# A two-block transformer step on one core: second halves of both output products taken block by block with their norms, router per block, first two gathers by the router's own row numbers

## The chip, the cores and the metric

One core of a Trainium2 chip runs the program. The metric is the time of one launch on the device in microseconds, as the median of the runs. TensorE multiplies, VectorE, ScalarE and GpSimd work on rows in SBUF, SyncE issues most of the loads.

## The reference

One sequence of 512 tokens, width 1024, in float32, goes through two different blocks. The first block mixes tokens by a gated linear attention and a state-space scan, multiplies by an output matrix and adds to the residual; then a root-mean-square norm (RMS norm) and a retrieval of single-neuron experts by product keys. The second block mixes by a short convolution and a forgetting attention, multiplies by an output matrix, adds; then a norm and a mixture of 32 experts with a router.

```python
h = h + mixed @ w_out                          # first output product
n2 = rmsnorm(h, norm_ffn_w)
h = h + peer_ffn(n2, ...)                      # starts with n2 @ w_query, 16 tiles of 128 features
...
x = x + token_mixer(rmsnorm_2(x, g_mix), ...)  # ends with m @ w_out_2, second output product
hf = rmsnorm_2(x, g_ffn)
pg = softmax(hf @ w_router_group); le = hf @ w_router_expert
x = x + hier_moe(hf, ...)                      # top 1 of 4 groups, top 2 of its 8 experts
```

## The kernel before, in words

The program is one instruction stream for each engine, written out by hand and held together by semaphores: the order on each engine is the order of its code, and an instruction whose semaphore is late holds up all behind it on the same engine.

**Numbers as pairs.** Float32 operands are split into a bf16 high half (ScalarE, a copy) and a bf16 low half (VectorE, operand minus high half). A product is three bf16 matmuls, high-high, high-low and low-high (`mm3`, L684 to L687).

**Weights.** All weights come as chunks of 1 MB (128 x 2048 float32), loaded by SyncE in the order of use into a ring of four slots `w_st`; ScalarE writes `w_hi` (L1176), VectorE `w_lo` (L1586), each up to three chunks ahead (`ahead(n)`), as the slot's last users allow (`used(n)`). In the expert stage the ring has twelve slots, some of them in buffers of earlier stages (`a_hi`, `a_lo`, `xn`), and the splits stand at L1505 and L2134. The loads into `a_hi` and `a_lo` wait for the router's last matmul, those into `xn` wait until GpSimd has read `xn` and both first gathers have landed.

**Tokens.** The 512 tokens are four blocks of 128. A token-major product (`token_tiles`, L701) covers 512 output columns for all four blocks with two chunks: for chunk 0 all four blocks, then for chunk 1 all four blocks, 12 matmuls of 512 columns each time. Each output product is two such halves. VectorE adds the result to the residual (L1759, L2108), and behind the second half each block is normalised: ScalarE square (L1186) and root (L1188), VectorE reciprocal (L1596) and scaling (L1600) into `xn`.

**Turning.** What follows wants features on the partitions. `transpose_rows` (L720, its matmul L730) turns a block with eight 128x128 transposes in two groups of four, each group in one of two PSUM banks; ScalarE writes the group's high half into `a_hi` (L1195), VectorE its low half into `a_lo` (L1610). A group waits until the bank's group before it is split (`tp_lo`). Before the change all four blocks are turned behind the whole product (uses 2 and 5), and the next product waits for all of them:

```python
token_tiles(C_WOUT + 2, 0, a_hi, a_lo)
transpose_rows(2)
pe.wait_ge(tp_lo, 3 * KT)
...
token_tiles(C_WO2 + 2, 4, m_split[:, :, 0, :], m_split[:, :, 1, :])
pe.drain().then_inc(moe_mm, RING)
transpose_rows(5)
pe.wait_ge(tp_lo, 6 * KT)
```

**Query stage.** Behind the first product come 16 query tiles (`feature_tile`, L689): each 24 matmuls over all 512 tokens, two tiles to a weight chunk, in banks 4 to 7 in turn. VectorE's low half is at L1824, ScalarE's high half at L1307.

**Router and gathers.** Behind the second product the router takes 24 matmuls of 36 columns for each block. GpSimd meanwhile stores each normalised block as a bf16 pair in DRAM (L618, L620, L622). VectorE picks experts, ranks the tokens and writes the row numbers of every expert, `row_i` (L2231). GpSimd waits for them, copies two columns to `idx` (L646), drains, and gathers 64 rows each for the first two experts (L626); TensorE turns the gathered rows (L1091) and starts on expert 0. Later gathers are issued one expert ahead, by `idx` (copies at L630).

Of the kernel before, what the change touches and what calls it, by code (L numbers as in the profile page):

```python
# [15 lines left out]
P = 128  # L16
# [110 lines left out]
def build_program(nc, w_all, x_in, cols_in, small_in, rows_in, out):  # L127
    ctx = ExitStack()
    with ctx:  # L129
# [340 lines left out]

        block = ctx.enter_context(nc.Block())
# [48 lines left out]
        def _(pool):  # L520
# [104 lines left out]
            def gather(p):  # L625
                pool.indirect_dma_start(x_g[0:CAP, p, :, :].rearrange("p a d -> p (a d)"), None, x_dram,  # L626
                                        bass.IndirectOffsetOnAxis(ap=idx[0:CAP, p:p + 1], axis=0)).then_inc(xe_ld[p], 16)
# [52 lines left out]
        def _(pe):  # L680
# [8 lines left out]
            def feature_tile(f, n, half, r_hi, r_lo, bank=None):  # L689
# [30 lines left out]
            def transpose_rows(use, by_block=True):  # L720

                for n in range(KT):
# [3 lines left out]
                    for m in range(4):  # L726
# [3 lines left out]
                        last = pe.transpose(ps[:, g % 2, m * P:(m + 1) * P], xn[:, tb, kt * P:(kt + 1) * P], ident[:, :])  # L730
# [148 lines left out]
            for m in range(2 * N_QUERY):  # L879
                feature_tile(F_QUERY + m, C_QUERY + m // 2, m % 2, a_hi, a_lo)  # L880
# [190 lines left out]
            last.then_inc(rt_mm, 1)  # L1071
# [95 lines left out]
        def _(act):  # L1167
# [22 lines left out]
            def transposed(use, weight=None, dst=a_hi, blocks=range(TB)):  # L1190

                for n in range(2 * blocks[0], 2 * blocks[-1] + 2):
                    act.wait_ge(tp_done, KT * use + n + 1)
                    if weight is None:
                        act.activation(dst[:, (n % 2) * 4:(n % 2) * 4 + 4, (n // 2) * P:(n // 2 + 1) * P],  # L1195
                                       ps[:, n % 2, :].rearrange("p (k t) -> p k t", k=4), ACT.Copy).then_inc(tp_hi, 1)
# [1176 lines left out]
```

## Time and profile before

| | us |
|---|---|
| median of the runs (2842.1 to 2848.28) | 2842.36 |
| the profiled execution | 2843.14 |
| its span, first to last instruction | 2841.5 |
| TensorE busy | 2652.2 (93%) |
| VectorE busy | 2021.4 (71%) |
| ScalarE busy | 1294.2 (46%) |
| GpSimd busy | 654.1 (23%) |

The profile is of one execution. Times are counted from the span's start; PE is TensorE's matmuls, PEld its weight loads, DVE VectorE, ACT ScalarE, POOL GpSimd, SP SyncE. Matmuls are pipelined: one that is shown with 0.38 us starts a good 0.2 us behind the one before, so their cost is the distance of their starts. In brackets stands how long the engine was idle before a row, and what ended that; "issue" is idle time for which the profile shows no wait.

### The profile page before, as it was taken

Reading aid. Unit: us, or ns where it says so; the run is one execution under the profiler, and the core shown is the slowest. Engines: PE = TensorE matmul, PEld = TensorE weight load, DVE = VectorE, ACT = ScalarE, POOL = GpSimd, SP = SyncE. Lnnn points to the kernel's source line nnn. Section 1 sums busy time; section 2 is a strip of 40 time slices with the busy share of each in tenths; the row PEclk is TensorE's granted clock in tenths of the full one; section 3 lists DMA queues with packets and bytes.
Section 4 is the critical chain, followed back from the end, with each engine's and each line's share of the span. In section 5 each row is a group of like instructions: output and inputs, shape, how many; then the busy total and the mean of one; then the engine's idle time right before and its main releaser. Section 6 shows DMA issues by size and latency. Waiting matters only on the chain. (4 is left out here: it accounts for less than half of the span.)

```text
span 2841.5 us, 39775 instructions
## 1 busy us (share of the span) xinstructions
PE 2652.2 (93%) x14118; PEld 1344.3 (47%) x14323; DVE 2021.4 (71%) x3310; ACT 1294.2 (46%) x1379; POOL 654.1 (23%) x480
## 2 busy tenths in 40 slices
PE   6988999999999999999999699999999599999994
PEld 3464444444455554444444344455554355555552
DVE  4544688886788885888888754366643588888885
ACT  5432323323444444333333333344431478888884
POOL 0000000000001013888888400000000332223221
PEclk9988999999999999999999899999999799999997
DMA  5201234443375658999999522212113399999994
GB/s 193 104 30 60 97 112 156 148 147 149 139 225 180 226 178 283 347 366 362 365 369 362 218 89 104 89 60 75 68 53 147 145 394 390 397 398 399 394 397 158
DMA packets 129053, 609.05 MB, mean 214 GB/s; under 512 B 17328, under 2 KB 33712, under 8 KB 79296
## 3 DMA queue, kind: packets, MB, share of 16 engines
q1 hardware_dynamic: 57312, 411.62, 38.3%
q0 software_dynamic: 45024, 149.00, 15.0%
q10 hardware_dynamic: 26624, 47.19, 4.9%
q8 instruction: 58, 0.95, 0.1%
q14 instruction: 35, 0.29, 0.0%
HBM read 539.59 MB, written 68.16 MB: 214 GB/s over the span
## 5 line engine op out<-in xcount | busy, mean ns | idle before, releaser
L686 PE MATMUL ps<-a_lo,w_hi 128*128 128x512 bf16 x1654 | 628.5, 380 | 6.3 <-DVE a_lo L1610 1.8
L687 PE MATMUL ps<-a_hi,w_lo 128*128 128x512 bf16 x1653 | 627.9, 380 | 1.4
L685 PE MATMUL ps<-w_hi,arena 128*128 128x512 bf16 (+1 forms) x1583 | 602.2, 380 | 16.3 <-ACT arena L1522 14.6
L685 PE MATMUL ps<-a_hi,w_hi 128*128 128x512 bf16 x1604 | 609.5, 380 | 2.4 <-ACT arena L1419 0.7
L686 PE MATMUL ps<-w_lo,arena 128*128 128x512 bf16 (+1 forms) x1582 | 601.4, 380 | 3.0 <-DVE arena L1945 2.2
L687 PE MATMUL ps<-w_hi,arena 128*128 128x512 bf16 (+1 forms) x1583 | 601.5, 380 | 0.9
L1834 DVE TENSOR_TENSOR w_lo<-w_st,w_hi 128x2048 bf16<-128x2048 f32 x128 | 293.2, 2290 | 184.0 <-ACT w_hi L1316 151.7
L1316 ACT ACTIVATE w_hi<-w_st 128x2048 bf16<-128x2048 f32 x128 | 244.4, 1909 | 321.8 <-PE ps L687 315.1
L590 POOL DMA_INDIRECT arena<-act_dram,h_idx x128 | 270.6, 2114 | 39.9 <-issue 39.9
L1322 ACT ACTIVATE xn<-ps 128x512 f32<-128x512 f32 x128 | 76.4, 597 | 426.8 <-PE ps L687 426.8
L1586 DVE TENSOR_TENSOR w_lo<-w_st,w_hi 128x2048 bf16<-128x2048 f32 x67 | 153.1, 2288 | 153.2 <-ACT w_hi L1176 152.9
L685 PEld LDWEIGHTS ps<-w_hi,arena 128*128 128x128 bf16 (+1 forms) x1600 | 166.2, 104 | 198.8 <-issue 17.7
L687 PEld LDWEIGHTS ps<-a_hi,w_lo 128*128 128x128 bf16 x1680 | 164.8, 98 | 199.3 <-issue 1.9
L685 PEld LDWEIGHTS ps<-a_hi,w_hi 128*128 128x128 bf16 x1680 | 164.9, 98 | 190.2 <-issue 4.1
L687 PEld LDWEIGHTS ps<-w_hi,arena 128*128 128x128 bf16 (+1 forms) x1600 | 166.4, 104 | 180.5 <-issue 1.7
L686 PEld LDWEIGHTS ps<-a_lo,w_hi 128*128 128x128 bf16 x1680 | 164.8, 98 | 182.9 <-issue 1.3
L686 PEld LDWEIGHTS ps<-w_lo,arena 128*128 128x128 bf16 (+1 forms) x1600 | 166.2, 104 | 176.6 <-issue 1.6
L566 POOL DMA_DIRECT2D act_dram<-xn x64 | 34.1, 533 | 752.3 <-ACT xn L1322 741.8
L1920 DVE TENSOR_SCALAR xn<-iota_b,arena 128x128 bf16<-128x128 bf16 x768 | 175.6, 312 | 0.0
L1176 ACT ACTIVATE w_hi<-w_st 128x2048 bf16<-128x2048 f32 x67 | 127.2, 1903 | 106.0 <-PE ps L687 106.0
L2134 DVE TENSOR_TENSOR w_lo<-w_st,w_hi 128x2048 bf16<-128x2048 f32 x64 | 145.9, 2282 | 28.0 <-ACT w_hi L1505 28.0
L2134 DVE TENSOR_TENSOR w_lo<-arena,w_hi 128x2048 bf16<-128x2048 f32 x64 | 144.7, 2281 | 4.2 <-ACT w_hi L1505 4.2
(392 smaller groups left out, 3749.8 us busy)
## 6 DMA issues: line engine op xcount, KB each, us to landing
w_st<-in_w_all SPq DMA_DIRECT2D x260, 1024.0 KB
arena<-in_w_all SPq DMA_DIRECT2D x64, 1024.0 KB
act_dram<-xn POOLq DMA_DIRECT2D x64, 512.0 KB, 2.9
xn<-in_w_all SPq DMA_DIRECT2D x32, 1024.0 KB, 9.1
arena<-act_dram ACTq DMA_DIRECT2D x64, 384.0 KB
gate_dram<-arena POOLq DMA_DIRECT2D x7, 3072.0 KB, 19.3
arena<-gate_dram ACTq DMA_DIRECT2D x64, 336.0 KB
a_hi<-in_w_all SPq DMA_DIRECT2D x16, 1024.0 KB, 9.1
```

The costliest lines, as they stand in the source:

```text
L566: pool.dma_start(act_dram[i * 8 + c], u_st[:, c % 2, :, :].rearrange("p j t -> p (j t)")).then_inc(u_stored[c % 2], 16)
L590: pool.indirect_dma_start(act_0[:, k:k + 1], None, acts, bass.IndirectOffsetOnAxis(ap=h_idx[:, k:k + 1], axis=0)).then_inc(act_ld[k // ROW ...
L685: pe.matmul(dst, l_hi, r_hi, start=start, stop=False)
L686: pe.matmul(dst, l_hi, r_lo, start=False, stop=False)
L687: return pe.matmul(dst, l_lo, r_hi, start=False, stop=stop)
L1176: act.activation(dst, w_st[:, n % RING, :], ACT.Copy).then_inc(w_hi_done, 1)
L1316: act.activation(w_hi[:, s, :], w_st[:, s, :], ACT.Copy).then_inc(w_hi_done, 1)
L1322: act.activation(u_st[:, c % 2, t, :], ps[:, t, :], ACT.Gelu).then_inc(u_out, 1)
L1586: dve.tensor_tensor(lo_n, w_st[:, n % RING, :], hi_n, ALU.subtract).then_inc(w_lo_done, 1)
L1834: dve.tensor_tensor(w_lo[:, s, :], w_st[:, s, :], w_hi[:, s, :], ALU.subtract).then_inc(w_lo_done, 1)
L1920: last = dve.tensor_scalar(oh_a[:, at % 2, r, part, :], iota_b[:, :], c_slot[:, 0, k:k + 1], c_slot[:, 2 + part, k:k + 1], ALU.is_equal, A ...
L2134: dve.tensor_tensor(w_lo[:, s, :], moe_st[k % MOE_RING], w_hi[:, s, :], ALU.subtract).then_inc(w_lo_done, 1)
```

## The change

The second half of each output product goes block by block (`block_tiles`): both chunks for block 0, then both for block 1, and so on, so both chunks are wanted from the start. The turns of finished blocks (`turn`) stand among them on TensorE. In the first product block 0 is turned behind block 2 and block 1 behind block 3, in banks 6 and 7 (`TURN_2`), and query tiles 0 and 1 are computed in parts: blocks 0 and 1 (256 columns), block 2, block 3, each when its block is split, with turn 3 in between. In the second product block 0 is turned behind block 1 and so on, and the router takes blocks 0 to 2 ahead of the turn of block 3. ScalarE and VectorE normalise each block before they split the turn of the block before it. Chunk C_WOUT + 6 = C_QUERY + 1 (query tiles 2 and 3) is no longer split ahead of the norms but behind the last turn. The bank of a query tile is 4 + m % 4 on ScalarE and VectorE too; `transposed` gets the argument `bank`. GpSimd's first pass gathers by `row_i` itself, without copy and drains, and drains once before the third gather's row numbers are used.

```diff
--- before
+++ after
@@ -643,11 +645,15 @@
 
             def first(r):
                 pool.wait_ge(rt_row, r + 1)
-                pool.tensor_tensor(idx[0:CAP, 0:2], row_i[0:CAP, 0:2], zero_i[0:CAP, :], ALU.add)
-                pool.drain()
-                gather(0)
-                gather(1)
-                pool.drain()
+                if isinstance(r, int):
+                    gather(0, row_i)
+                    gather(1, row_i)
+                else:
+                    pool.tensor_tensor(idx[0:CAP, 0:2], row_i[0:CAP, 0:2], zero_i[0:CAP, :], ALU.add)
+                    pool.drain()
+                    gather(0)
+                    gather(1)
+                    pool.drain()
                 next_rows(0, 2)
                 pool.drain()
...
@@ -686,17 +692,35 @@
                 pe.matmul(dst, l_hi, r_lo, start=False, stop=False)
                 return pe.matmul(dst, l_lo, r_hi, start=False, stop=stop)
 
-            def feature_tile(f, n, half, r_hi, r_lo, bank=None):
+            def feature_tile(f, n, half, r_hi, r_lo, bank=None, cols=slice(0, T), done=True):
 
                 chunk(n)
                 if bank is None and f >= 4:
                     pe.wait_ge(ft_out, f - 3)
-                dst = ps[:, 4 + f % 4 if bank is None else bank, :]
+                dst = ps[:, 4 + f % 4 if bank is None else bank, cols]
                 for kt in range(KT):
                     w = slice(half * D + kt * P, half * D + (kt + 1) * P)
-                    last = mm3(dst, w_hi[:, n % RING, w], w_lo[:, n % RING, w], r_hi[:, kt, :], r_lo[:, kt, :],
+                    last = mm3(dst, w_hi[:, n % RING, w], w_lo[:, n % RING, w], r_hi[:, kt, cols], r_lo[:, kt, cols],
                                kt == 0, kt == KT - 1)
-                last.then_inc(ft_done, 1)
+                if done:
+                    last.then_inc(ft_done, 1)
+
+            def block_tiles(n, bank, l_hi, l_lo, tb):
+
+                rows = slice(tb * P, (tb + 1) * P)
+                for part in range(2):
+                    if tb == 0:
+                        chunk(n + part)
+                    for k in range(4):
+                        kt = part * 4 + k
+                        w = slice(k * 512, (k + 1) * 512)
+                        last = mm3(ps[:, bank + tb, :], l_hi[:, kt, rows], l_lo[:, kt, rows],
+                                   w_hi[:, (n + part) % RING, w], w_lo[:, (n + part) % RING, w],
+                                   kt == 0, kt == KT - 1)
+                    if part == 1:
+                        last.then_inc(tok_done, 1)
+                    elif tb == TB - 1:
+                        last.then_inc(tok_half, 1)
 
             def token_tiles(n, bank, l_hi, l_lo, split=None, before=0):
...
@@ -861,11 +885,30 @@
             pe.wait_ge(ssd_yd, TB)
             transpose_rows(1, by_block=False)
             token_tiles(C_WOUT, 4, a_hi, a_lo, tp_lo, KT)
-            token_tiles(C_WOUT + 2, 0, a_hi, a_lo)
-
-
-            transpose_rows(2)
+
+            def turn(use, tb, bank=0):
+                transpose_rows(use, groups=range(2 * tb, 2 * tb + 2), bank=bank)
+
+            for tb in range(TB):
+                block_tiles(C_WOUT + 2, 0, a_hi, a_lo, tb)
+                if tb >= 2:
+                    turn(2, tb - 2, TURN_2)
+
+            def query_part(m, blocks):
+                first, end = blocks
+                feature_tile(F_QUERY + m, C_QUERY + m // 2, m % 2, a_hi, a_lo, 4 + m % 4, slice(first * P, end * P), end == TB)
+
+            turn(2, 2, TURN_2)
+            pe.wait_ge(tp_lo, 2 * KT + 4)
+            query_part(0, (0, 2))
+            query_part(1, (0, 2))
+            turn(2, 3, TURN_2)
+            pe.wait_ge(tp_lo, 2 * KT + 6)
+            query_part(0, (2, 3))
+            query_part(1, (2, 3))
             pe.wait_ge(tp_lo, 3 * KT)
+            query_part(0, (3, 4))
+            query_part(1, (3, 4))
 
             def scores(unit, h, rows):
 
@@ -876,8 +919,10 @@
                                keys_hi[:, q, :], keys_lo[:, q, :], True, True)
                 last.then_inc(s_done, 1)
 
-            for m in range(2 * N_QUERY):
-                feature_tile(F_QUERY + m, C_QUERY + m // 2, m % 2, a_hi, a_lo)
+            for m in range(2, 2 * N_QUERY):
+                if m >= 4:
+                    pe.wait_ge(ft_out, F_QUERY + m - 3)
+                query_part(m, (0, 4))
                 if m % 2 and 3 <= m < 3 + 2 * EARLY:
                     pe.wait_ge(ft_out, F_QUERY + m - 1)
...
@@ -1057,18 +1102,25 @@
                     pe.wait_ge(mix_done, j - 1)
                 feature_tile(ao_out(j) - 1, C_AO + j, 1, c_hi, c_lo, bank=7 - 2 * (j % 2))
             token_tiles(C_WO2, 0, m_split[:, :, 0, :], m_split[:, :, 1, :], mix_lo)
-            token_tiles(C_WO2 + 2, 4, m_split[:, :, 0, :], m_split[:, :, 1, :])
-
-            pe.drain().then_inc(moe_mm, RING)
-
-            transpose_rows(5)
-            pe.wait_ge(tp_lo, 6 * KT)
             for tb in range(TB):
+                block_tiles(C_WO2 + 2, 4, m_split[:, :, 0, :], m_split[:, :, 1, :], tb)
+                if tb == TB - 1:
+                    pe.drain().then_inc(moe_mm, RING)
+                if tb:
+                    turn(5, tb - 1)
+
+            def router(tb):
+                pe.wait_ge(tp_lo, 5 * KT + 2 * tb + 2)
                 for kt in range(KT):
                     rows, w = slice(tb * P, (tb + 1) * P), slice(O_R + kt * SM_R, O_R + (kt + 1) * SM_R)
                     last = mm3(ps[:, 2, tb * SM_R:(tb + 1) * SM_R], a_hi[:, kt, rows], a_lo[:, kt, rows], small_hi[:, w], small_lo[:, w],
                                kt == 0, kt == KT - 1)
-            last.then_inc(rt_mm, 1)
+                return last
+
+            for tb in range(TB - 1):
+                router(tb)
+            turn(5, TB - 1)
+            router(TB - 1).then_inc(rt_mm, 1)
 
             pe.wait_ge(rt_pick, 1)
             pe.matmul(ps[:, 3, 0:TB * NE].rearrange("p (t e) -> p t e", e=NE), tri_le[:, :], e_any, start=True, stop=False)
...
@@ -1290,21 +1342,20 @@
                 act.drain()
             act.activation(sd[:, 0:TB * SG], ss[:, 0:TB * SG], ACT.Sqrt, scale=1.0 / (SJ * SP_), bias=eps[:, :]).then_inc(ssd_sd, 1)
             transposed(1, lambda kt: col("gla_norm") if kt < 4 else col("ssd_norm", kt - 4))
-            for g in range(2):
-                ahead(C_WOUT + 2 * g)
-                act.wait_ge(tok_half, G_WOUT + g + 1)
-                ahead(C_WOUT + 2 * g + 1)
+            ahead(C_WOUT)
+            act.wait_ge(tok_half, G_WOUT + 1)
+            ahead(C_WOUT + 2)
 
 
             for tb in range(TB):
-                if tb == TB - 1:
-                    transposed(2, blocks=[0])
                 norm(1, tb, res_done, tb + 1)
-            transposed(2, blocks=range(1, TB))
+                if tb:
+                    transposed(2, blocks=[tb - 1], bank=TURN_2)
+            transposed(2, blocks=[TB - 1], bank=TURN_2)
             for m in range(2 * N_QUERY):
...
@@ -1752,20 +1802,16 @@
 
             for g in range(2):
                 ahead(C_WOUT + 2 * g)
-                ahead(C_WOUT + 2 * g + 1)
                 for tb in range(TB):
                     dve.wait_ge(tok_done, TB * (G_WOUT + g) + tb + 1)
                     s = slice(g * 512, (g + 1) * 512)
                     last = dve.tensor_tensor(res[:, tb, s], res[:, tb, s], ps[:, 4 - 4 * g + tb, :], ALU.add)
                     if g == 1:
                         last.then_inc(res_done, 1)
+                        normalise(1, tb)
                         if tb:
-                            normalise(1, tb - 1)
-            transposed(2, blocks=[0])
-            normalise(1, TB - 1)
-
-
-            transposed(2, blocks=range(1, TB))
+                            transposed(2, blocks=[tb - 1], bank=TURN_2)
+            transposed(2, blocks=[TB - 1], bank=TURN_2)
             def best_keys(h):
 
```

ScalarE's and VectorE's parts for the second product are changed in the same way as those shown for the first.

## Rows read from the trace of the kernel before

**Rows 1.** Waits of TensorE, 2190 to 2257 us: us in total, times, longest
```profile
PE ps L1091 <- DMA arena<-x_dram,arena: 12.5, 1, 12.5
```

**Rows 2.** Windows: busy us of PE, PEld, DVE, ACT, POOL; granted clock; DMA share; GB/s
```profile
284.90:308.50 23.60, 17.68 (x80) 9.74 (x80) 13.84 (x16) 10.21 (x15) 3.76 (x7) 0.78 0.30 112
...
2243.30:2257.40 14.10, 1.03 (x16) 0.87 (x16) 2.98 (x4) 1.19 (x2) 4.15 (x4) 0.50 0.12 37
2300.00:2400.00 100.00, 97.39 (x570) 50.62 (x569) 88.79 (x53) 81.56 (x66) 29.74 (x18) 1.00 1.01 392
2700.00:2800.00 100.00, 93.80 (x538) 48.43 (x536) 87.03 (x52) 79.35 (x63) 16.57 (x12) 1.00 0.83 326
```

**Rows 3.** Timeline of TensorE behind the first output product: start, us, line, operation
```profile
284.93 1.04 PE L730 MATMUL ps<-ident,xn 128*128 128x128 f32 x8
...
290.77 1.97 PE L730 MATMUL ps<-ident,xn 128*128 128x128 f32 x8 [1.60 <-DVE a_lo L1610]
...
297.08 0.63 PE L686 MATMUL ps<-a_lo,w_hi 128*128 128x512 bf16 x1 [1.82 <-DVE a_lo L1610]
297.50 0.63 PE L687 MATMUL ps<-a_hi,w_lo 128*128 128x512 bf16 x1
...
308.34 0.38 PE L687 MATMUL ps<-a_hi,w_lo 128*128 128x512 bf16 x1
308.56 0.38 PE L685 MATMUL ps<-a_hi,w_hi 128*128 128x512 bf16 x1
```

**Rows 4.** Timeline of VectorE in the same stretch
```profile
276.79 2.29 DVE L1586 TENSOR_TENSOR w_lo<-w_st,w_hi 128x2048 bf16<-128x2048 f32 x1 [8.09 <-ACT w_hi L1176]
...
285.13 0.69 DVE L1759 TENSOR_TENSOR res<-res,ps 128x512 f32<-128x512 f32 x1 [0.31 <-PE ps L687]
285.74 0.16 DVE L1596 RECIPROCAL rstd<-sd 128x1 f32<-128x1 f32 x1
285.97 1.28 DVE L1600 SCALAR_TENSOR_TENSOR xn<-res,rstd,row 128x1024 f32<-128x1024 f32 x1
...
295.93 0.69 DVE L1610 TENSOR_TENSOR a_lo<-ps,a_hi 128x512 bf16<-128x512 f32 x1 [0.16 <-ACT a_hi L1195]
```

**Rows 5.** Timeline of ScalarE in the same stretch
```profile
286.54 1.06 ACT L1186 ACTIVATE xn<-res 128x1024 f32<-128x1024 f32 x1
...
287.75 0.29 ACT L1188 ACTIVATE sd<-ss,eps 128x1 f32<-128x1 f32 x1
...
294.44 0.60 ACT L1195 ACTIVATE a_hi<-ps 128x512 bf16<-128x512 f32 x1 [1.08 <-PE ps L730]
...
295.79 3.70 ACT L1176 ACTIVATE w_hi<-w_st 128x2048 bf16<-128x2048 f32 x2
```

**Rows 6.** Timeline of TensorE: router's first and last matmul, the first expert's rows
```profile
2226.69 0.19 PE L685 MATMUL ps<-small_hi,a_hi 128*128 128x36 bf16 x1 [1.42 <-DVE a_lo L1610]
...
2229.24 0.20 PE L687 MATMUL ps<-small_hi,a_lo 128*128 128x36 bf16 x1
...
2255.57 1.03 PE L1091 MATMUL ps<-ident_b,arena 64*128 64x64 bf16 x16 [12.47 <-DMA arena<-x_dram,arena]
```

**Rows 7.** Timeline of VectorE: block 3's rows, the row numbers, the next chunk's low half
```profile
2217.29 2.84 DVE L1600 SCALAR_TENSOR_TENSOR xn<-res,rstd,row 128x1024 f32<-128x1024 f32 x1
...
2243.14 0.18 DVE L2231 CAST arena<-ps 64x32 int32<-64x32 f32 x1 [0.55 <-PE ps L1141]
2243.25 2.27 DVE L2134 TENSOR_TENSOR w_lo<-w_st,w_hi 128x2048 bf16<-128x2048 f32 x1
```

**Rows 8.** Timeline of GpSimd: the program's first gather, then the expert stage
```profile
1103.85 1.04 POOL L594 DMA_INDIRECT arena<-in_w_all,v_idx  x1 [0.31 <-issue]
...
2243.41 2.16 POOL L646 TENSOR_TENSOR arena<-arena,zero_i 64x2 int32<-64x2 int32 x1 [11.86 <-DVE arena L2231]
2251.69 0.95 POOL L626 DMA_INDIRECT arena<-x_dram,arena  x1 [6.12 <-issue]
...
2287.21 2.80 POOL L626 DMA_INDIRECT arena<-x_dram,arena  x1 [0.16 <-issue]
```

More of the change, by code:

```diff
@@ L623, in _, with gather @@
             pool.wait_ge(x_st, 16 * TB)
-            def gather(p):
+            def gather(p, rows=idx):
                 pool.indirect_dma_start(x_g[0:CAP, p, :, :].rearrange("p a d -> p (a d)"), None, x_dram,
-                                        bass.IndirectOffsetOnAxis(ap=idx[0:CAP, p:p + 1], axis=0)).then_inc(xe_ld[p], 16)
+                                        bass.IndirectOffsetOnAxis(ap=rows[0:CAP, p:p + 1], axis=0)).then_inc(xe_ld[p], 16)
             def next_rows(i, c):
@@ L718, in token_tiles, with transpose_rows @@
                             last.then_inc(tok_half, 1)
-            def transpose_rows(use, by_block=True):
-                for n in range(KT):
+            def transpose_rows(use, by_block=True, groups=range(KT), bank=0):
+                for n in groups:
                     g = KT * use + n
@@ L729, in transpose_rows @@
                             pe.wait_ge(xn_done, TB * use + tb + 1)
-                        last = pe.transpose(ps[:, g % 2, m * P:(m + 1) * P], xn[:, tb, kt * P:(kt + 1) * P], ident[:, :])
+                        last = pe.transpose(ps[:, bank + g % 2, m * P:(m + 1) * P], xn[:, tb, kt * P:(kt + 1) * P], ident[:, :])
                     last.then_inc(tp_done, 1)
@@ L1188, in norm, with transposed @@
                 act.activation(sd[:, tb:tb + 1], ss[:, tb:tb + 1], ACT.Sqrt, scale=1.0 / D, bias=eps[:, :]).then_inc(sd_done, 1)
-            def transposed(use, weight=None, dst=a_hi, blocks=range(TB)):
+            def transposed(use, weight=None, dst=a_hi, blocks=range(TB), bank=0):
                 for n in range(2 * blocks[0], 2 * blocks[-1] + 2):
@@ L1486, in _ @@
             mix_high(KT - 1)
-            for g in range(2):
-                ahead(C_WO2 + 2 * g)
-                act.wait_ge(tok_half, G_WO2 + g + 1)
-                ahead(C_WO2 + 2 * g + 1)
+            ahead(C_WO2)
+            act.wait_ge(tok_half, G_WO2 + 1)
+            ahead(C_WO2 + 2)
             for tb in range(TB):
-                if tb == TB - 1:
-                    transposed(5, blocks=[0])
                 norm(4, tb, res_done, TB + tb + 1)
-            transposed(5, blocks=range(1, TB))
+                if tb:
+                    transposed(5, blocks=[tb - 1])
+            transposed(5, blocks=[TB - 1])
             def hi_of(r, i, k):
@@ L1602, in normalise, with transposed @@
                     dve.drain().then_inc(row_used, 1)
-            def transposed(use, weight=None, dst_hi=a_hi, dst_lo=a_lo, blocks=range(TB)):
+            def transposed(use, weight=None, dst_hi=a_hi, dst_lo=a_lo, blocks=range(TB), bank=0):
                 for n in range(2 * blocks[0], 2 * blocks[-1] + 2):
@@ L1609, in transposed @@
                         part = (slice(None), slice((n % 2) * 4, (n % 2) * 4 + 4), slice((n // 2) * P, (n // 2 + 1) * P))
-                        dve.tensor_tensor(dst_lo[part], ps[:, n % 2, :].rearrange("p (k t) -> p k t", k=4), dst_hi[part], ALU.subtract).then_inc(tp_lo, 1)
+                        dve.tensor_tensor(dst_lo[part], ps[:, bank + n % 2, :].rearrange("p (k t) -> p k t", k=4), dst_hi[part], ALU.subtract).then_inc(tp_lo, 1)
                     else:
@@ L2103, in _ @@
                 ahead(C_WO2 + 2 * g)
-                ahead(C_WO2 + 2 * g + 1)
                 for tb in range(TB):
@@ L2110, in _ @@
                         last.then_inc(res_done, 1)
+                        normalise(4, tb)
                         if tb:
-                            normalise(4, tb - 1)
-            transposed(5, blocks=[0])
-            normalise(4, TB - 1)
-            transposed(5, blocks=range(1, TB))
+                            transposed(5, blocks=[tb - 1])
+            transposed(5, blocks=[TB - 1])
             def rows_of_pass(r):
```

7 lines of the change are left out of this document (4 added, 3 removed).

## The prediction

> **What bounds the kernel now.** TensorE is busy for 93% of the span (table above), so I began with who waited for whom on it, in the two stretches that change. The longest wait there is 12.5 us, for the rows of the first gather [rows 1]; the others are of a few us each, for the low halves of transposed rows. Next I took the windows [rows 2]. From the end of the first output product to query tile 2 TensorE is busy 17.7 of 23.6 us at a mean granted clock of 0.78; between the router's row numbers and the first expert TensorE is busy 1.03 of 14.1 us, and the DMA share is 0.12: nothing else runs there either. Between 2300 and 2400 TensorE is 97% busy and the DMA engines are full too, but between 2700 and 2800 the DMA share is already 0.83 with TensorE still busy, so the weight stream is done ahead of TensorE and the expert stage goes by TensorE. All stages hang on the one before by semaphores only. What is saved in either place is therefore saved at the end, if the next wait doesn't take it.
>
> **First place: the first output product.** A turn is the eight transposes of one block of 128 tokens. Durations: a 512-column matmul at the high level (2.4 GHz, granted clock 1.00) starts every 0.216 us; at the low level (1.2 GHz, 0.50) every 0.427 us; eight transposes take 1.04 us, 1.97 at the low level [rows 3]. One block of the second half is 24 matmuls, 5.18 us; the four blocks cost 20.7 us in either order. VectorE: residual add 0.69 (the next starts after 0.61), reciprocal and its drain 0.23, normalise 1.28, low half of a transposed group 0.69, low half of a weight chunk 2.29 [rows 4]. ScalarE: from the square to the end of the root 1.50, high half of a group 0.60, two chunks' high halves 3.70, so 1.9 each [rows 5].
> Before: the transposes start at 284.93, directly behind the product, query tile 0 at 296.65 (one matmul ahead of the 297.08 in the row), and tile 2 at 308.56 [rows 3]. The gap is 11.7 us, two of the four turns at the low level; and tiles 0 and 1 take 11.9 us where 48 matmuls at 0.216 are 10.4, so 1.5 us more went to the low level.
> After, from the start of the second half at 264.4: blocks 0 to 2 end at 279.9, turn 0 at 281.0, block 3 at 286.2, turn 1 at 287.2. VectorE is the queue to follow: it takes the residual add of block 2 only after turn 0 has been split (282.4), and that of block 3 only after turn 1 has (288.7). Turn 2 waits for turn 1's buffers: 288.1 to 289.2. The residual of block 3 is ready at 289.3, its root at 290.95, its rows at 292.5, turn 2's low half at 293.7. Meanwhile TensorE does the 256-column parts of query tiles 0 and 1: 2 x 2.6 us, 289.2 to 294.4. Turn 3: 294.4 to 295.5. The third blocks' parts (2 x 1.3): to 298.1; turn 3 is split at 296.9, so the last parts follow without a wait to 300.8. Narrow matmuls cost by their columns: 96 matmuls of 36 columns, each with a new stationary tile, take 2.55 us [rows 6], so setting one costs no more than 0.027 us and hides under 128 columns.
> The weight chunk of tiles 2 and 3 was split under the product before (276.79 in [rows 4]); now it is split after turn 3: high half 296.1 to 298.0, low half to 300.4. That is 0.4 us ahead of need: I cost it at nothing, and its cover is thin. The two chunks behind it come under tiles 2 and 3; SyncE's load of the chunk five later goes out some 21 us later than before, and is needed only at tile 10. Gain: 308.56 - 300.8 = **7.8 us**. Bounds: no more than 8.7 (TensorE without any wait: 20.7 + 4.2 + 10.6 us); no less than 3 (the four last short parts at the low level, 2 us each later or so, and the chunk late).
>
> **Second place: the second output product and the router.** The second half starts at 2192.5. Before, its 20.7 us end at 2213.3 and the router's 96 matmuls run from 2226.69 to 2229.44 [rows 6]; their result is read right behind. VectorE normalised block 3 at 2217.29 for 2.84 instead of 1.28 us [rows 7], beside a GpSimd subtraction.
> After: turns 0 and 1 stand among the blocks, +2.1 us, block 3 ends at 2215.5. Its residual 2216.1, root 2217.9, rows at 2219.5 (GpSimd is in the store of block 2 by then, so 1.28 and not 2.84), turn 2's low half 2220.75. TensorE has turned block 2 and done the router of blocks 0 and 1 by 2218.1 and waits; router 2 ends at 2221.5, turn 3 at 2222.5 to 2223.4 by the clock, its low half 1.4 us later, the last router block takes 0.65 to 0.8. The result is whole at 2225.0 (2224.6 to 2225.8). Gain: **4.4 us**, bounds 2.5 (block 3's rows slow again, and the low level) and 5.5. GpSimd's four stores start earlier and are out by 2226; the row numbers come some 13 us later, so that wait stays hidden. The 14 us of routing arithmetic are untouched.
>
> **Third place: the gathers.** Before, the row numbers are written at 2243.32 (2243.14 + 0.18), GpSimd copies them (2.16 us), its drain and what follows leave it idle for 6.12 us, and the first gather is issued at 2251.69 for 0.95 us; TensorE starts on the gathered rows at 2255.57, that is 2.93 us after the first issue ended [rows 6 to 8]. Now the gathers read the row numbers themselves. Ahead of gathers elsewhere the idle time is 0.31 us after a wait [rows 8]. But VectorE starts a chunk's low half at 2243.25 for 2.27 us [rows 7], and a gather in the expert loop, issued beside such subtractions, takes 2.80 us instead of 0.95 [rows 8]. So: issue ends 2.3 + 0.9 = 3.2 us after the row numbers, not 9.3. Gain **6.1 us**; bounds 8.0 (no such lengthening) and 0 (the idle time just moves ahead of the gather, and the lengthening comes on top). The copy for the third gather comes after both, and that gather isn't needed for two experts. SyncE's loads into xn wait for both gathers; the second then lands some 6 us earlier as well, so the stream shifts with TensorE. Its lead at the end [rows 2] covers the rest.
> The trace's 6.12 us has a rule that speaks against this part. The Trainium skill, "GPSIMD Engine Reference", section Instruction dispatch, says that the first call to a freshly loaded GpSimd kernel additionally pays a load of about 6 us with no visible instruction; by it the idle time would belong to the gather and stay. The trace doesn't decide: at 1103.85 the first of all gathers waited only 0.31 us, but it followed other DMA work and not arithmetic [rows 8].
>
> **Sum.** 7.8 + 4.4 + 6.1 = 18.3 us. The profiled execution took 2843.14 us, 0.8 above the median: 2843.1 - 18.3 = 2824.8 against it, and 2824.0 against the median. What a measurement of this kernel can tell from no change is about 0.3%, 8.5 us.
>
> **Rivals.**
> (a) The 6 us ahead of the first gather stay. GpSimd would wait 2.16 us less (the copy), VectorE's subtraction would be over, so only about 2.2 us are gained there: 7.8 + 4.4 + 2.2 = 14.4, 2828. For it: nothing that the profile names fills the 6.12 us. Against: the gather at 1103.85, and the later gathers behind a copy wait only 0.16 us [rows 8]. By the skill's rule just named it would go so. 20%.
> (b) The deferred chunk split isn't covered: ScalarE takes it behind turn 3 and TensorE waits some 4 us before tile 2. 14 us in all, 2828. For it: a margin of 0.4 us. Against: every duration in that chain is measured, and one would have to be off by several us. 10%.
> (c) Only the last block counts. Its own chain (residual, norm, turn, split, router) stays as long as it was, and the two turns among the blocks come on top, in both places (2 x 2.1 us): 6.1 - 4.2, no more than 2 us gained, 2840.5, no change. For it: the end of both products is set by block 3 alone. Against: that chain was 16 us long while its own links, summed from [rows 4 to 6], are about 8; the rest was other blocks' work queued in front on ScalarE and VectorE. 6%.
> (d) Slower: the short parts with waits between them leave TensorE at the low level, and it stays there in the query stage. Each 512-column matmul then costs 0.211 us more; from 87 of them (under four tiles) the whole gain is gone, from 127 the kernel is measurably slower; over all 16 query tiles it is 384 x 0.211 = 81 us, less the 18: 2905. For it: turn 2 went at the low level 6 us after turn 0 had gone at the high one [rows 3]. Against: tiles 0 and 1 lost only 1.5 us to it before it was back [rows 3], and after the change there is less idle time, not more. 4%.
>
> **Numbers.** Forecast as summed 60%, (a) 20%, (b) 10%, (c) 6%, (d) 4%. Faster by over 0.3%: 0.90; within 0.3%: 0.06; slower by over 0.3%: 0.04. Range: the bounds of the three terms taken one at a time reach from 2822 to 2830, all three at their best give 2820; (a) and (b) lie inside, and both at once give 2832. So 2820 to 2832.
>
> **What would show it.** Right: one 8-transpose group between blocks 2 and 3 near 280 at 1.04 us; query tile 2 starts near 300.8, directly behind tile 1's last part, at 0.216 us spacing throughout; the router's last matmul near 2217.2 (2225.0 less the 7.8 gained before); the first gather starts under 0.5 us after the row numbers are written and takes near 2.8 us; the expert stage keeps its length. Wrong: a GpSimd idle time of about 6 us ahead of the first gather (a); TensorE idle before tile 2 until w_lo (b); TensorE idle for over 8 us between block 3's end and the last router block (c); a granted clock of 0.50 after 302 (d); or, if expert waits now name w_lo or a weight load, the stream was the bound.

## The result, and the profile after

| | before | after |
|---|---|---|
| median of the runs, us | 2842.62 (2842.1 to 2848.28) | 2827.72 (2825.69 to 2829.11) |
| ratio | | 0.9944 [0.993, 0.9957] |
| the profiled execution, us | 2843.14 | 2825.69 |
| its span, us | 2841.5 | 2823.9 |

The median before includes the runs made beside the changed kernel. The 27 runs of the kernel before beside the first experiments lie in two groups, near 2842.5 and near 2847.6 us, so a difference of two medians is good to a few us only, and the terms are better read from traces. The change gains 14.9 us by the medians and 17.45 us between the two profiled executions; the one profiled after is the fastest of its four. The forecast was 2824.0, in a range of 2820 to 2832.

The page's busy times, after:

```profile
span 2823.9 us, 39964 instructions
...
PE 2648.8 (94%) x14215; PEld 1348.0 (48%) x14419; DVE 2019.6 (72%) x3310; ACT 1293.6 (46%) x1379; POOL 651.2 (23%) x479
```

TensorE does nearly the same work (2648.8 against 2652.2 us busy). So the time is idle time that went, and it has to be found by place.

**Where the 17.6 us of the span went.** I took the same events in both traces and subtracted. Each figure is how much earlier the event comes after the change:

| event | before | after | earlier by |
|---|---|---|---|
| last residual add of the first product's first half | 264.41 | 263.85 | 0.56 |
| high half of query tile 2 copied | 313.94 | 305.20 | 8.74 |
| first tile of the retrieval loop | 387.46 | 378.72 | 8.74 |
| last tile of the retrieval loop | 1102.12 | 1095.07 | 7.05 |
| last residual add of the second product's first half | 2192.59 | 2185.16 | 7.43 |
| router's result read | 2229.47 | 2218.06 | 11.41 |
| row numbers written | 2243.32 | 2231.92 | 11.40 |
| TensorE starts on the gathered rows | 2255.57 | 2237.88 | 17.69 |
| end | 2841.50 | 2823.95 | 17.55 |

The first place gives 8.74 - 0.56 = 8.2 us, the second 11.41 - 7.43 = 4.0, the third 17.69 - 11.40 = 6.3, in all 18.5. The 0.56 is no part of the three: the four other kernels with the first product as it was show the same add at 263.1 to 265.9 us. Between the first and the last tile of the retrieval loop, in code that the change doesn't touch, 1.7 us are lost.

**First place.** TensorE from block 2's end to query tile 2, the timeline that answers to [rows 3]:

```profile
279.19 1.04 PE L754 MATMUL ps<-ident,xn 128*128 128x128 f32 x8
...
285.24 1.04 PE L754 MATMUL ps<-ident,xn 128*128 128x128 f32 x8
...
287.26 1.25 PE L754 MATMUL ps<-ident,xn 128*128 128x128 f32 x8 [0.98 <-DVE a_lo L1660]
288.35 0.27 PE L691 MATMUL ps<-a_hi,w_hi 128*128 128x256 bf16 x1
...
293.59 1.04 PE L754 MATMUL ps<-ident,xn 128*128 128x128 f32 x8
...
299.76 0.22 PE L693 MATMUL ps<-a_hi,w_lo 128*128 128x128 bf16 x1
300.04 0.38 PE L692 MATMUL ps<-a_lo,w_hi 128*128 128x512 bf16 x1
```

The first two rows are turns 0 and 1 among the blocks, 1.04 us each. Turn 2 waits 0.98 us for its banks, the 256-column parts run from 288.35, turn 3 goes at the high level, and query tile 2 starts at 299.8 (one matmul ahead of the row at 300.04), without an idle time between. VectorE in the same stretch, answering to [rows 4]:

```profile
286.51 1.29 DVE L1660 TENSOR_TENSOR a_lo<-ps,a_hi 128x512 bf16<-128x512 f32 x2 [1.07 <-ACT a_hi L1247]
287.71 0.68 DVE L1808 TENSOR_TENSOR res<-res,ps 128x512 f32<-128x512 f32 x1
...
290.21 1.28 DVE L1650 SCALAR_TENSOR_TENSOR xn<-res,rstd,row 128x1024 f32<-128x1024 f32 x1
...
297.14 6.70 DVE L1636 TENSOR_TENSOR w_lo<-w_st,w_hi 128x2048 bf16<-128x2048 f32 x3 [1.00 <-ACT w_hi L1228]
```

Turn 1 is split and only then comes block 3's residual add (287.71). The row at 297.14 is three weight chunks' low halves one behind the other: the first, which tile 2 needs and whose split was put off, ends a third of the way in, at 299.4. The windows, in the columns of [rows 2], first the turning, then the stretch between the row numbers and the first expert, then the two stretches of the expert stage:

```profile
264.00:299.60 35.60, 34.52 (x267) 22.54 (x267) 20.92 (x25) 16.12 (x24) 3.77 (x7) 1.00 0.22 75
...
2232.00:2239.60 7.60, 1.03 (x16) 0.88 (x16) 2.77 (x3) 1.07 (x2) 3.88 (x3) 0.50 0.25 69
2300.00:2400.00 100.00, 97.39 (x569) 50.66 (x568) 88.79 (x54) 81.58 (x66) 29.84 (x18) 1.00 1.01 396
```

TensorE is busy for 34.5 of 35.6 us at a granted clock of 1.00; before, the turning alone went at 0.78 [rows 2]. The expert stage is as it was.

**Second place.** TensorE in the second product, answering to the first rows of [rows 6]:

```profile
2208.18 1.07 PE L754 MATMUL ps<-ident,xn 128*128 128x128 f32 x8 [0.26 <-issue]
2209.09 0.18 PE L691 MATMUL ps<-small_hi,a_hi 128*128 128x36 bf16 x1
...
2213.24 0.19 PE L691 MATMUL ps<-small_hi,a_hi 128*128 128x36 bf16 x1 [2.79 <-DVE a_lo L1660]
2213.86 1.85 PE L754 MATMUL ps<-ident,xn 128*128 128x128 f32 x8
...
2217.12 0.21 PE L691 MATMUL ps<-small_hi,a_hi 128*128 128x36 bf16 x1 [1.42 <-DVE a_lo L1660]
...
2217.83 0.20 PE L693 MATMUL ps<-small_hi,a_lo 128*128 128x36 bf16 x1
```

TensorE waits 2.79 us for block 2's low half, and turn 3 then takes 1.85 us instead of 1.04: most of it went at the low level.

**Third place.** GpSimd and, below it, TensorE, answering to [rows 8] and [rows 6]:

```profile
2232.19 2.75 POOL L628 DMA_INDIRECT arena<-x_dram,arena  x1 [13.77 <-DVE arena L2273]
2235.25 0.93 POOL L628 DMA_INDIRECT arena<-x_dram,arena  x1 [0.30 <-issue]
```

```profile
2237.88 1.03 PE L1143 MATMUL ps<-ident_b,arena 64*128 64x64 bf16 x16 [6.18 <-DMA arena<-x_dram,arena]
```

The first gather starts 0.27 us after the row numbers are written; the 6.12 us of [rows 8] have not moved ahead of it. It takes 2.75 us, beside this row of VectorE:

```profile
2231.85 2.27 DVE L2176 TENSOR_TENSOR w_lo<-w_st,w_hi 128x2048 bf16<-128x2048 f32 x1
```

TensorE's wait for the rows is 6.2 us instead of 12.5 [rows 1].

**Where the 1.7 us went.** The stretch of 4 us at the entry to the retrieval loop, before the change and after it, columns as above:

```profile
384.00:388.00 4.00, 2.59 (x16) 1.45 (x18) 1.13 (x2) 3.73 (x3) 0.00 (x0) 1.00 0.52 219
```

```profile
377.00:381.00 4.00, 3.77 (x11) 1.52 (x12) 2.26 (x2) 2.99 (x2) 0.00 (x0) 0.58 0.13 53
```

The granted clock falls to 0.58 on average, and about eight matmuls start 0.427 us apart instead of 0.216: 8 x 0.211 = 1.7 us. The idle time ahead of it, a wait of 1.93 us before the change and 1.94 after it, is in both traces.

### The profile page after: what moved, and what is told of

Same layout as the page of the kernel before. It is cut to its first block and busy times, and to the rows that moved or that the text cites. A ratio compares the mean times of both kernels' runs of the same rounds, so it can differ in the third digit from the quotient of the medians.

```text
span 2823.9 us, 39964 instructions
## 1 busy us (share of the span) xinstructions
PE 2648.8 (94%) x14215; PEld 1348.0 (48%) x14419; DVE 2019.6 (72%) x3310; ACT 1293.6 (46%) x1379; POOL 651.2 (23%) x479
## 5 line engine op out<-in xcount | busy, mean ns | idle before, releaser
L692 PE MATMUL ps<-a_lo,w_hi 128*128 128x512 bf16 (+2 forms) x1686 | 632.2, 376 | 4.5 <-issue 0.7
L693 PE MATMUL ps<-a_hi,w_lo 128*128 128x512 bf16 (+2 forms) x1686 | 632.0, 376 | 1.4
L691 PE MATMUL ps<-a_hi,w_hi 128*128 128x512 bf16 (+2 forms) x1636 | 613.4, 376 | 2.4 <-ACT arena L1470 0.7
```

What stands on the lines that cost most here:

```text
L691: pe.matmul(dst, l_hi, r_hi, start=start, stop=False)
L692: pe.matmul(dst, l_hi, r_lo, start=False, stop=False)
L693: return pe.matmul(dst, l_lo, r_hi, start=False, stop=stop)
```

## The experiments

Three things were to be settled: whether the three terms are those of the three parts and add up; what the 6.12 us ahead of the first gather are; and whether the query parts or the turns among the blocks carry the first term.

**The change again**, five rounds, with no edit, to see what repeats.

> The changed kernel once more, with five rounds. By its one trace the three places gain 8.2, 4.0 and 6.3 us, 18.5 together, and 1.7 us are lost where TensorE enters the expert-retrieval loop at the lower clock for some 3.5 us, which the kernel before did not show. Theory: that loss is a matter of the single execution, so the trace of this run may show it or not, the three gains repeat within 0.3 us, and the median of more runs lies 15 to 18 us below the kernel before. Rival: the loss comes with the change every time; then this trace shows the clock at 0.5 near 378 us again and the median stays near 15 us below.

Measured: 2826.21 us (2825.51 to 2830.8, five runs); ratio 0.9942 [0.9929, 0.9956]. The trace repeats each term: 8.2, 4.0 and 6.3, and the 1.7 us lost at the loop's entry:

```profile
377.30:381.30 4.00, 3.84 (x10) 1.45 (x12) 2.38 (x2) 2.87 (x2) 0.00 (x0) 0.57 0.05 20
```

The expectation isn't settled by it: the loss was there again, as its rival says, and the median is 17.1 us below that of the kernel before (2843.35 beside these runs), as its theory says.

**The first product's part alone.** The kernel before with only these edits (and those of ScalarE and VectorE that belong to use 2):

```diff
-            token_tiles(C_WOUT + 2, 0, a_hi, a_lo)
-            transpose_rows(2)
+            for tb in range(TB):
+                block_tiles(C_WOUT + 2, 0, a_hi, a_lo, tb)
+                if tb >= 2:
+                    turn(2, tb - 2, TURN_2)
...
+            query_part(0, (0, 2))
+            query_part(1, (0, 2))
+            turn(2, 3, TURN_2)
...
```

> Only the first output product with its norms, turns and split query tiles is changed. Theory (the places add up): query tile 2 starts 8.2 us earlier, the second product's router and the gathers keep their length, 2834 to 2836 us in all. Rival (a stall moves: later stages are held by something else): tile 2 starts earlier but the time is within 3 us of the kernel before.

Measured: 2836.32 us (2835.68 to 2841.54, ten runs), ratio 0.9977 [0.9968, 0.9986]. In the trace query tile 2 comes 8.98 us earlier, of which 0.80 stand upstream: 8.2. The router and the gathers keep their length. The 1.7 us at the loop's entry are lost here too, and the median lies 0.3 us above the range that was expected.

**The second product's part alone.**

```diff
-            token_tiles(C_WO2 + 2, 4, m_split[:, :, 0, :], m_split[:, :, 1, :])
-            pe.drain().then_inc(moe_mm, RING)
-            transpose_rows(5)
...
+                block_tiles(C_WO2 + 2, 4, m_split[:, :, 0, :], m_split[:, :, 1, :], tb)
+                if tb == TB - 1:
+                    pe.drain().then_inc(moe_mm, RING)
+                if tb:
+                    turn(5, tb - 1)
...
+            for tb in range(TB - 1):
+                router(tb)
+            turn(5, TB - 1)
+            router(TB - 1).then_inc(rt_mm, 1)
```

> Only the second output product and the router are changed. Theory: the router's result is read 4.0 us earlier, the row numbers and gathers follow unchanged, 2838 to 2839 us. Rival (only the last block's chain counts, and two turns stand in front of it): no gain or 2 us slower, 2842 to 2845 us.

Measured: 2838.85 us (2837.98 to 2844.91, ten runs), ratio 0.9984 [0.9975, 0.9994]. In the trace the router's result comes 5.19 us earlier, 1.14 of them upstream: 4.05. The loop's entry goes at a clock of 1.00, as before the change:

```profile
384.00:388.00 4.00, 3.61 (x20) 1.90 (x22) 1.55 (x1) 3.69 (x3) 0.00 (x0) 1.00 0.30 123
```

**The gathers' part alone.**

```diff
-                pool.tensor_tensor(idx[0:CAP, 0:2], row_i[0:CAP, 0:2], zero_i[0:CAP, :], ALU.add)
-                pool.drain()
-                gather(0)
-                gather(1)
-                pool.drain()
+                if isinstance(r, int):
+                    gather(0, row_i)
+                    gather(1, row_i)
...
```

> Only the first two gathers take the router's row numbers directly; all else as before. Theory: the first gather starts 0.3 us after the row numbers instead of 8.4, takes 2.75 us instead of 0.95 beside VectorE's subtraction, and TensorE starts on its rows 6.3 us earlier: 2836 us. Rival (the idle time belongs to the gather's first call and was gone in the changed kernel for another reason, the earlier stores): 6 us of idle time ahead of the first gather, 2840 us.

Measured: 2838.72 us (2834.92 to 2841.41, ten runs), ratio 0.9975 [0.9966, 0.9985]. The profiled execution reaches the row numbers 4.2 us late, in code that the edit doesn't touch, and TensorE starts on the rows 2.06 us early, so the part gives 6.24 us:

```profile
2247.78 2.75 POOL L626 DMA_INDIRECT arena<-x_dram,arena  x1 [11.78 <-DVE arena L2235]
```

The 4.2 us can be placed: 1.45 are lost up to the first product's first half, 1.3 more up to query tile 2, where the low level lasts longer than in [rows 2] (0.71 over the same 23.6 us, instead of 0.78), and 1.7 at the loop's entry; 0.3 come back behind it.

```profile
286.35:309.95 23.60, 17.88 (x74) 9.48 (x74) 13.84 (x16) 10.22 (x15) 3.76 (x7) 0.71 0.30 112
```

The three parts alone give 8.2 + 4.05 + 6.24 = 18.5 us, what the whole change shows in the same places. They neither help nor hinder one another. By the medians, against 2843.35 us, they gain 7.0, 4.5 and 4.6 us, 16.1 together, and the whole change 17.1. The 1.7 us are lost here as well, and this kernel has the first product as it was: the loss can come without the first part.

**What are the 6.12 us?** Three theories were held against one another: C, the copy as GpSimd's first arithmetic of its kind; G, the first gather itself; D, the drain between them, which has to wait for something that the transfers issued before have left. The first test adds a copy of the same kind to the kernel before, into a tile of its own, while GpSimd waits for the row numbers:

```diff
+            pool.tensor_tensor(warm[0:CAP, :], zero_i[0:CAP, :], zero_i[0:CAP, :], ALU.add)
+
             def first(r):
```

> The kernel before, with one more GpSimd copy of the same form (64 x 2, int32, into a tile nobody reads) while GpSimd waits for the row numbers. Where do the 6 us ahead of the first gather come from? Theory C (a first call of the integer copy is cold): the copy is warm now, and the first gather starts 5 to 6 us earlier, near 2.7 us after the row numbers. Theory D (the drain waits by itself, for what the transfers issued since the last drain left behind): no change, the first gather starts 8.4 us after the row numbers. Theory G (the first gather after arithmetic is cold): no change either.

The second adds a drain at the same spot instead:

```diff
+            pool.drain()
+
             def first(r):
```

> The kernel before, with one more GpSimd drain, alone, while GpSimd waits for the row numbers. Theory D: the early drain takes the 5 us, hidden; the drain behind the copy then ends with the copy, and the first gather starts some 3 us after the row numbers instead of 8.4. Theories C and G: no change, 8.4 us.

GpSimd with the early copy:

```profile
2230.46 0.18 POOL L645 TENSOR_TENSOR warm<-zero_i 64x2 int32<-64x2 int32 x1
2242.11 2.17 POOL L649 TENSOR_TENSOR arena<-arena,zero_i 64x2 int32<-64x2 int32 x1 [11.47 <-DVE arena L2234]
2250.40 0.95 POOL L627 DMA_INDIRECT arena<-x_dram,arena  x1 [6.12 <-issue]
```

and with the early drain:

```profile
2241.88 2.16 POOL L648 TENSOR_TENSOR arena<-arena,zero_i 64x2 int32<-64x2 int32 x1 [11.65 <-DVE arena L2233]
2244.83 0.95 POOL L626 DMA_INDIRECT arena<-x_dram,arena  x1 [0.79 <-issue]
```

The early copy changes nothing: 6.12 us again, 2842.08 us in its one run. The early drain takes the 6.12 us down to 0.79, TensorE starts on the rows 6.9 us after the row numbers instead of 12.25, and the one run took 2835.71 us. In the trace's records of single instructions the early drain itself lasts from 2230.11 for 5.50 us, though the block stores, the last transfers before it, had landed by 2230.1; the drain behind the copy then ends 0.06 us after the copy. So it is the drain, the first one behind issued transfers, and not the copy or the gather. The copy's 2.17 us aren't its own either: the same copy without VectorE beside it took 0.18.

What of theory D isn't shown is its reason, that the transfers left something to wait for. GpSimd's drains behind gathers later in these traces end 0.07 to 0.13 us after the last gather has landed (before the change: landed at 2257.06, drain over at 2257.19), with no 5.4 us on top. Only the first one takes them; 343 transfers had been issued ahead of it. Whether it is their number, or that it is the first drain behind any, no run tells apart. Nor do the 5.4 us seem to be gone after the change: its first drain now stands behind the two gathers and the copy of the third row number and ends at 2242.16, 2.8 us after the second gather has landed and 5.8 us after the copy, where no one on the critical path waits for it.

**A drain ahead of the first gather**, in the changed kernel:

```diff
                 if isinstance(r, int):
+                    pool.drain()
                     gather(0, row_i)
```

> The changed kernel with one drain put back ahead of the first gather, and no copy. Theory D: the first gather starts 5 to 6 us after the row numbers instead of 0.3, and takes 0.95 us since VectorE's subtraction is over. Theory C: under 1 us. Theory G: under 1 us, since no arithmetic stands between.

```profile
2243.47 0.95 POOL L628 DMA_INDIRECT arena<-x_dram,arena  x1 [19.73 <-issue]
```

The row numbers are written at 2237.33 here, so the gather starts 6.14 us after them instead of 0.27, with no copy between: the drain a second time (its record lasts 5.38 us). The one run took 2834.95 us; TensorE starts on the rows 9.3 us later than in the repeat, of which 5.2 us were lost before the edit, nearly all of it in two places (2.1 up to the first product's first half, 3.2 between the convolution and the second product).

**Query tiles 0 and 1 whole, behind all four turns**, in the changed kernel:

```diff
             turn(2, 2, TURN_2)
-            pe.wait_ge(tp_lo, 2 * KT + 4)
-            query_part(0, (0, 2))
-            query_part(1, (0, 2))
             turn(2, 3, TURN_2)
...
             pe.wait_ge(tp_lo, 3 * KT)
-            query_part(0, (3, 4))
-            query_part(1, (3, 4))
+            query_part(0, (0, 4))
+            query_part(1, (0, 4))
```

> The changed kernel, but query tiles 0 and 1 are computed whole, behind the last turn. Theory: most of the first place's 8.2 us come from these parts, because they fill TensorE while block 3 is normalised: tile 2 starts 5.5 to 7 us later than in the changed kernel, 2832 to 2834 us. Rival: block order and early turns carry the gain, and the parts bring under 2 us.

Measured: 2833.67 us (2832.13 to 2836.36, five runs), ratio 0.9959 [0.9945, 0.9973]. TensorE's timeline:

```profile
289.99 1.25 PE L754 MATMUL ps<-ident,xn 128*128 128x128 f32 x8 [0.98 <-DVE a_lo L1654]
...
295.11 1.97 PE L754 MATMUL ps<-ident,xn 128*128 128x128 f32 x8 [3.87 <-DVE a_lo L1654]
...
298.50 0.61 PE L691 MATMUL ps<-a_hi,w_hi 128*128 128x512 bf16 x1 [1.41 <-DVE a_lo L1654]
```

Between turn 2 and turn 3 TensorE has nothing to do for 3.87 us, turn 3 and the first matmuls of tile 0 then go at the low level, and tile 2's copy comes 49.04 us behind the first half's last add instead of 41.35. So the parts carry 7.7 of the 8.2 us, a little more than the 5.5 to 7 that were expected: that two turns stand among the blocks is worth little by itself.

**The chunk's low half behind the first expert's rows**, in the changed kernel. This takes VectorE's subtraction away from beside the first gather:

```diff
-                lo_of(r, 0, 1)
                 rows_lo(r, 0, 0)
+                lo_of(r, 0, 1)
```

> The changed kernel, but VectorE splits chunk 1 of the first expert behind the low half of the first gathered rows, not right behind the row numbers. Theory (VectorE's subtraction holds GpSimd up while it issues the gather): the first gather takes 0.95 us instead of 2.75, and TensorE starts on its rows 1.8 us earlier, 2824.5 us. Rival: the 2.75 us are the gather's own, nothing moves.

```profile
2232.14 0.95 POOL L628 DMA_INDIRECT arena<-x_dram,arena  x1 [13.74 <-DVE arena L2273]
```

```profile
2236.07 1.03 PE L1143 MATMUL ps<-ident_b,arena 64*128 64x64 bf16 x16 [4.42 <-DMA arena<-x_dram,arena]
```

Measured: 2823.14 us (2822.78, 2822.96, 2823.32, 2825.74), ratio 0.9921 [0.9906, 0.9936]. The gather takes 0.95 instead of 2.75 us, and TensorE starts 4.2 us after the row numbers instead of 5.96 (5.92 in the repeat). The subtractions now stand behind the rows' low halves (4.48 us for two chunks at 2237.75) and cost nothing of it: the first expert's output comes 2.5 us earlier than in the change, counted from the row numbers. This version is the fastest of all: its median is 3.1 us below the repeat's, though the slowest of its four runs lies beside the fastest of the repeat's five. (The kernel before had a median of 2847.63 us beside these runs, so the ratio can't be set against those above.)

**Two more moves on top of that one**: the turn of a block directly behind the next block in the first product too, and turn 3 ahead of the router of block 2.

```diff
-                if tb >= 2:
-                    turn(2, tb - 2, TURN_2)
+                if tb:
+                    turn(2, tb - 1, TURN_2)
...
-            turn(2, 2, TURN_2)
...
-            for tb in range(TB - 1):
+            for tb in range(TB - 2):
                 router(tb)
             turn(5, TB - 1)
+            router(TB - 2)
```

> The changed kernel with three more edits: the later split of split_later (1.8 us), the turn of block 3 ahead of the router's block 2 in the second product (1.0 us), and in the first product block 0 turned behind block 1 and so on, as in the second, so that VectorE isn't held by a turn when block 3 is ready (1.2 us). Theory: 4 us less than the changed kernel, 2822 to 2823 us. Rival: the earlier work only waits elsewhere, under 2 us.

```profile
2214.68 1.34 PE L754 MATMUL ps<-ident,xn 128*128 128x128 f32 x8 [2.20 <-DVE a_lo L1660]
```

Measured: 2824.4 us (2823.94 to 2824.53, five runs), ratio 0.9922 [0.9908, 0.9935]: not below the version before it, and above the 2822 to 2823 that were expected. Its places do what was asked. The first is 1.35 us shorter (40.00 instead of 41.35 from the first half's last add to tile 2's copy), the second 1.7 us (31.17 instead of 32.87), and the loop's entry loses nothing. But it reaches the first product 2.3 us late and loses 3.2 us between the convolution and the second product. By the trace's records of the clock TensorE stands at the low level there for 17.1 us instead of 10.2, and half of the difference is 3.4 us. Two windows of that stretch, first of the version before it, then of this one, then of the kernel with the drain, which loses the same (the boundary between the two isn't the same instruction in each, so compare the clock and not the lengths):

```profile
1650.00:2048.00 398.00, 388.75 (x2107) 206.90 (x2105) 210.73 (x357) 164.19 (x256) 0.00 (x0) 1.00 0.23 83
2048.00:2098.00 50.00, 43.71 (x244) 26.56 (x245) 23.19 (x53) 16.88 (x29) 0.00 (x0) 0.93 0.12 43
```

```profile
1649.00:2050.00 401.00, 390.03 (x2107) 207.22 (x2104) 212.37 (x358) 164.11 (x256) 0.00 (x0) 0.99 0.23 82
2050.00:2100.00 50.00, 45.43 (x243) 27.19 (x244) 21.41 (x52) 16.81 (x29) 0.00 (x0) 0.90 0.12 43
```

```profile
1652.00:2053.00 401.00, 390.31 (x2107) 207.27 (x2105) 212.28 (x357) 164.29 (x256) 0.00 (x0) 0.99 0.23 82
2053.00:2103.00 50.00, 45.18 (x242) 26.96 (x243) 21.46 (x52) 16.54 (x29) 0.00 (x0) 0.90 0.12 43
```

The kernel with the drain has the changed kernel's code all through this stretch, is as late at the first product (2.1 us against the repeat), and shows the same clock here (0.90 near 2075). So the last edits aren't needed for such a loss. Whether they make it more frequent is open: all five runs lie within 0.6 us of one another, and one was traced.

## Why the prediction was right, point by point

- **First place**, 7.8 forecast, 8.2 measured. Turn 2's start was put at 288.1, turn 3's at 294.4 and tile 2's at 300.8; they came at 287.3, 293.6 and 299.8. 0.56 us of that is upstream. The weight chunk, costed at nothing with 0.4 us to spare, was ready 0.4 us ahead of need, so its cover held and rival (b) didn't come. What carried the term was the query parts, by 7.7 of 8.2 us. The clock stayed at 1.00 over the whole stretch, and rival (d) didn't come.
- **Second place**, 4.4 forecast, 4.0 measured: a size slightly off. The term that was mis-sized is "turn 3 at 2222.5 to 2223.4 by the clock": the sum took the middle, and of the two levels left open the low one came, 1.85 us for the turn. Block 3's rows took 1.28 us, as forecast. The last router matmul was put near 2217.2 and came at 2217.83.
- **Third place**, 6.1 forecast, 6.3 measured. The issue beside the subtraction took 2.75 us (forecast about 2.8) and started 0.27 us after the row numbers (under 0.5). Rival (a), the 6 us staying ahead of the gather, didn't come. The prediction had left open what they are; the two early tests show it: GpSimd's drain, the first behind issued transfers. By the rule of the Trainium skill, "GPSIMD Engine Reference", section Instruction dispatch, a first call to a freshly loaded kernel pays some 6 us for loading; here neither the early copy (6.12 us stayed) nor the first gather (0.27 us after its wait) shows it. Whether the first drain's 5.4 us are such a first call, no run shows. The price of the rival was right for a gather that keeps a drain ahead of it (6.14 us), and the change takes just that drain away. Here the forecast was partly lucky: it took the 6.12 us as gone without knowing what they were.
- **Only the last block counts**, rival (c): it would have left at most 2 us in the two products; 12.2 were measured.
- **The sum.** 18.3 forecast, 18.5 in the three places. What failed is the step that all else keeps its length: the entry to the retrieval loop lost 1.7 us to a low clock, in a stretch without an edit, and 0.56 came for nothing upstream; with small rests that is the 17.55 of the two traces. The median of 2827.72 (2826.21 in the repeat) is 2 to 4 us above the forecast. The 1.7 us are in it; the rest, executions that took up to 5 us more than the traced one, has no trace and stays open, though the losses seen elsewhere (2.1 and 3.2 us) are of that size.

The 1.7 us aren't the change's own work, but the kernel may meet them more often with it. Of the traces at hand, before, the second part alone, the whole tiles, the two kernels with an early copy or drain and the last one don't have the loss; the change, its repeat, the first part alone, the gathers alone, the drain ahead of the gather and the later split do. So all five traces with the changed kernel's first product, uncut, have it, and one of the five with the old one (before, the second part alone, the gathers alone, the early copy, the early drain). The gathers alone, edited only 1800 us further on, show that the new order isn't needed for the loss; the count suggests that it comes more often with it. Where it does, 6.5 of the first place's 8.2 us are left. What decides it wasn't found.

## What to carry to other kernels

Where a product is followed by a norm, a turn and another product, look for work of the next product that needs only the finished blocks: here cutting two query tiles by block gave 7.7 of 8.2 us, and moving the turns alone 0.5. On GpSimd, keep the first drain behind issued transfers (5.4 us) off the path to a critical gather, by reading the finished data directly or by draining once while the engine waits anyway; a later one behind gathers costs the time until they have landed. And keep large VectorE subtractions away from the moment a critical gather is issued.

## What the runs showed of the hardware that was not expected

- The first GpSimd drain behind issued transfers took 5.4 to 5.5 us though the transfers had landed, alone (5.38 and 5.50 us) or counted from the end of the copy ahead of it (5.4 us before the change), and a second one behind it, with no transfer between, next to nothing: the idle time there fell from 6.12 to 0.79 us. Drains behind gathers further on ended 0.07 to 0.13 us after the landing.
- GpSimd's work is held up by the VectorE subtraction beside it (2.27 us): a copy of 64x2 numbers took 2.17 us instead of 0.18, a gather's issue 2.75 instead of 0.95, and taking the subtraction away gave the 0.95 back.
- Equal code with an equal wait ahead of it (1.93 us) was followed by a granted clock of 0.5 for some 3.5 us in some traces and by 1.00 in others, which cost 1.7 us. Two other losses in equal code were of 2.1 us (up to the first product) and 3.2 us (between the convolution and the second product, at the low level for 17.1 us instead of 10.2). That is as much as the smaller steps of such a change, so that terms under about 3 us have to be read from the traces place by place and not from the total.
